# Five blocks of on-chip buffers change places: the same tiles at other byte offsets

## The reference

```python
x   = x + 0.5 * m_x[2] * swiglu(modulate(rmsnorm(x, norm_g[0]), m_x[0], m_x[1]), ffn1_w1, ffn1_w2)
ctx = ctx + 0.5 * m_c[2] * swiglu(modulate(rmsnorm(ctx, norm_g[0]), m_c[0], m_c[1]), ffn1_w1, ffn1_w2)
px = modulate(rmsnorm(x, norm_g[1]), m_x[3], m_x[4]) @ w_in      # q, k, v, gate, u, vg
pc = modulate(rmsnorm(ctx, norm_g[1]), m_c[3], m_c[4]) @ w_in    # only k, v are used
ret = retention_readout(bidir_retention(rope(q), rope(k), v, states from ctx), gate)
gm  = gelu(u) * (W_s @ layernorm(gelu(vg)) + b_s)                # per chunk of 128 tokens
x = x + m_x[5] * (concat([ret, gm]) @ w_out)
x = x + 0.5 * m_x[8] * swiglu(modulate(rmsnorm(x, norm_g[2]), m_x[6], m_x[7]), ffn2_w1, ffn2_w2)
out = rmsnorm(x, final_g)
```

## Time and profile before

| | us |
|---|---|
| median of three runs | 2045.24 |
| profiled execution, its own time | 2042.7 |
| its span, first to last instruction | 2040.9 |
| TensorE busy in the span | 1998.3 (98%) |
| VectorE busy | 1268.1 (62%) |
| ScalarE busy | 758.4 (37%) |
| GpSimd busy | 497.5 (24%) |
| mean granted TensorE clock | 0.992 of full |

### The profile page before, as it was taken

One profiled execution on the slowest core, in us unless ns is written; L12 is line 12 of the kernel. 1 busy time (PEld: TensorE's weight loads), 2 busy tenths in 40 slices (PEclk: granted clock), 3 DMA queues, 4 the chain that ended last, 5 costly groups with the idle time before them and its releaser, 6 DMA issues.

```text
span 2040.9 us, 26021 instructions
## 1 busy us (share of the span) xinstructions
PE 1998.3 (98%) x10112; PEld 1691.4 (83%) x10112; DVE 1268.1 (62%) x1887; ACT 758.4 (37%) x1098; POOL 497.5 (24%) x311
## 2 busy tenths in 40 slices
PE   8999999999999998999999999999999999999997
PEld 5999988888888887888989898877788888888886
DVE  5987766556788678676454324468556555555555
ACT  4333533333333344445121221445333333334342
POOL 1000033333212204014223232555333421220001
PEclk9999999999999999999999999999999999999998
DMA  8874426666555786833101011121666644466664
GB/s 330 343 267 147 155 78 230 203 194 234 201 189 213 262 297 193 268 113 117 42 21 42 31 42 62 62 83 57 201 196 222 212 155 160 160 216 192 192 194 155
DMA packets 108762, 343.52 MB, mean 168 GB/s; under 512 B 11488, under 2 KB 20960, under 8 KB 90464
## 3 DMA queue, kind: packets, MB, share of 16 engines
q1 hardware_dynamic: 108640, 341.85, 49.1%
HBM read 267.36 MB, written 74.45 MB: 167 GB/s over the span
## 4 chain that ended last, share of the span: by engine, by line
PE 85%; issue 5%; DVE 5%; ACT 2%; DMA 1%; POOL 1%; SPq 0%; DVEq 0%; POOLq 0%; ACTq 0%
PE PS L2146 12%; PE PS L2147 12%; PE PS L2148 12%; PE PS L1988 8%; PE PS L1989 8%; PE PS L1990 8%; PE PS L2188 5%; PE PS L2189 5%; PE PS L2190 5%; PE PS L2104 4%; DVE WVL L1579 1%; PE PS L2364 1%; PE PS L2045 1%; DMA WR<-w_units 1%; DVE DG L1328 1%
## 5 line engine op out<-in xcount | busy, mean ns | idle before, releaser
L2146 PE MATMUL PS<-HH,WVH 128*128 128x512 f32 x672 | 262.5, 391 | 0.0
L2148 PE MATMUL PS<-HH,WVL 128*128 128x512 f32 x672 | 261.6, 389 | 0.0
L2147 PE MATMUL PS<-HL,WVH 128*128 128x512 f32 x672 | 261.5, 389 | 0.0
L1988 PE MATMUL PS<-HH,WH 128*128 128x512 f32 x416 | 164.9, 396 | 2.7 <-DVE WL L1770 2.7
L1990 PE MATMUL PS<-HH,WL 128*128 128x512 f32 x416 | 162.0, 389 | 0.0
L1989 PE MATMUL PS<-HL,WH 128*128 128x512 f32 x416 | 161.9, 389 | 0.0
L1579 DVE TENSOR_TENSOR WVL<-WR,WVH 128x512 fp32r<-128x512 f32 x160 | 115.5, 722 | 69.3 <-ACT WVH L1006 67.8
L2148 PEld LDWEIGHTS PS<-HH,WVL 128*128 128x128 f32 x672 | 126.1, 188 | 26.5
L2146 PEld LDWEIGHTS PS<-HH,WVH 128*128 128x128 f32 x672 | 126.2, 188 | 26.3 <-ACT U L1038 0.4
L2147 PEld LDWEIGHTS PS<-HL,WVH 128*128 128x128 f32 x672 | 126.2, 188 | 25.9
L1625 DVE TENSOR_TENSOR HL<-HLF,HH 128x1024 fp32r<-128x1024 f32 x76 | 106.0, 1404 | 60.0 <-ACT HH L1054 59.4
(11 more groups left out here) (282 smaller groups left out, 4933.6 us busy)
## 6 DMA issues: line engine op xcount, KB each, us to landing
WR<-w_units SPq DMA_DIRECT2D x89, 1024.0 KB, 5.7
gated<-HB SPq DMA_DIRECT2D x44, 512.0 KB, 6.6
down_weight_sums<-WB SPq DMA_DIRECT2D x22, 1024.0 KB, 3.8
gated_sums<-TBF SPq DMA_DIRECT2D x22, 768.0 KB, 4.2
AW<-ada_units SPq DMA_DIRECT2D x12, 1024.0 KB, 13.3
HLF<-down_weight_sums SPq DMA_DIRECT2D x46, 256.0 KB, 3.3
W2RB<-w_units SPq DMA_DIRECT2D x22, 512.0 KB, 3.6
WB<-w_units SPq DMA_DIRECT2D x22, 512.0 KB, 3.6
```

Of the source, the lines that this page charges most:

```text
L1988: pe.matmul(dst, wh, xh, start=first, stop=False)
L2146: pe.matmul(bank[:, :], wh, xh, start=first, stop=False, skip_group_check=True)
L2147: pe.matmul(bank[:, :], wh, xl, start=False, stop=False, skip_group_check=True)
L2148: ins = pe.matmul(bank[:, :], wl, xh, start=False, stop=k == 3, skip_group_check=True)
```

## The change

The five blocks are placed in another order. Nothing else differs: no instruction, no wait, no transfer, no size. The whole diff:

```diff
@@ -158,8 +158,7 @@
         def at(name, shape, dt, offset):
             return nc.alloc_sbuf_tensor_at(name, shape, dt, offset=offset)
 
-        R = 192
-        top = [R + 77824]
+        top = [192]
 
         def keep(name, shape, dt):
             n = 4 * int(np.prod(shape[1:]))
@@ -167,10 +166,7 @@
             top[0] += n
             return at(name, shape, dt, top[0] - n)
 
-        HIGHS = top[0]
-        HH = keep("HH", [P, KT, SEQ], F32R)
-        LOWS = top[0]
-        HL = keep("HL", [P, KT, SEQ], F32R)
+        X = keep("X", [P, KT, SEQ], F32)
         W = top[0]
         WR = keep("WR", [P, 2, KT, UC], F32)
         WH = keep("WH", [P, 2, KT, UC], F32R)
@@ -191,7 +187,12 @@
         LG = keep("LG", [P, 8], F32)
         IDX = keep("IDX", [P, Z_END], F32)
         Z = keep("Z", [P, 8, Z_END], F32)
-        X = keep("X", [P, KT, SEQ], F32)
+        R = top[0]
+        top[0] += 77824
+        LOWS = top[0]
+        HL = keep("HL", [P, KT, SEQ], F32R)
+        HIGHS = top[0]
+        HH = keep("HH", [P, KT, SEQ], F32R)
```

## The result

The changed kernel takes 2046.61 us (median of 20 runs, 2043.59 to 2048.88); the kernel before, run beside it, takes 2043.13 us (20 runs, 2040.36 to 2046.26). The ratio is 1.0014 with an interval of 1.0008 to 1.0020: slower by 2.9 us of 2043 (1.6 to 4.1). The forecast was no change. The profiled execution took 2048.38 us with a span of 2046.6 us, 5.7 us longer than the span of the earlier trace rows. An execution that fell to a far lower granted clock (one of `b64ctx` at 2229.66 us, one of the kernel before beside it at 2501.26 us) is in no ratio.

What follows compares the result with a forecast made beforehand. TensorE was taken as the bound, busy for 1998.3 of 2040.9 us. TensorE's pace, other engines and transfers summed as 0 + 0 + 0 on the median, giving 2045.2 us, range 2041.0 to 2049.5 us.

Steps and rivals of the forecast that it cites:

- the first term of the sum: TensorE's pace in ring and mixer: same step at all homes, taken as 0, at most 3.0 us either way.
- Three ways only, and TensorE's pace is one of them: Time can change only by TensorE's pace, other engines' instructions on the chain (143 us), or transfers there (some 20 us).
- Another step, by even 1 ns, breaks the first term and is worth 10 us: Check on ring and mixer: matmul starts must stay 226.7 to 226.9 ns apart.
- The other engines, 0: ScalarE's splits (1060 ns) and VectorE's low parts (1225 ns) keep their lengths; 0, at most 1.4 us either way.
- The transfers, 0: Loads on the chain land as before, WR in 5.6 to 5.8 us; 0, near bound 0.5 us, far 7.2 us.
- The pair of `gated` loads: Check on transfers: the 256 KB loads into the 76 KB block and HL land within 0.2 us of each other.
- The wait of the block period: TensorE's wait for `U<-U,PS`, 5 times and 4.0 us before; expected between 3 and 8 times.
- the two rivals that live there: Block period: slower, more waits, 2050.4 to 2054.8 us, chance 0.06; faster, waits go, 2041.2 us, chance 0.04.
- the transfers' one: Rival: all loads on the chain take 42% longer, 7.2 us, 2052.4 us; chance 0.03.
- The end of SBUF: Rival: HH reaches into space set aside for DMA descriptors, slowing its accesses; 3.0 us, 2048.2 us; chance 0.01.
- The clock: One half-speed stretch of 6.8 us more or less costs 3.4 us, about the three runs' spread of 3.3 us.

Runs made afterwards that it cites:

- b64ctx: Kernel before with the W block and the context's tiles in R each 64 bytes higher; 2048.64 us against 2044.25, ratio 1.0018.
- a64: Changed kernel with R, HL and HH 64 bytes further, so they differ from W by 0 modulo 256; ratio 1.0000 to the kernel before.
- atail: Changed kernel with the 3,520 bytes of small tables moved to the very end, behind HH; ratio 1.0002 to the kernel before.
- r64: Kernel before with 64 bytes left free between R and everything else; 2051.42 us against 2043.30, ratio 1.0042.
- m1_steps: Micro kernel without the layer: 48 fp32r matmuls at each of 21 weight offsets, 512 and 256 columns; 226.7 to 234.4 and 113.3 to 120.0 ns a step.

## Why the prediction was wrong

**The step that failed is the first term of the sum**: "Three pairings of homes at distances from zero to over 100,000 bytes have one pace ... I take 0: the nearest rows are equal." The rows were right and the conclusion wasn't. In all three pairings of the earlier trace rows the blocks' bases were 192 modulo 4096 and the operands inside them begin at multiples of 512 bytes: the distances varied by tens of thousands of bytes, but only in multiples of 512. The rows could not say anything on low address bits, and the change moved just these for one block. The table of offsets ahead of the prediction holds the hint: 32,960 minus 85,632 is no multiple of 256, while every difference of the bases `R`, `HIGHS`, `LOWS` and `W` before is. The size of the term was then capped by the reading error of the stretches, 0.3 ns a step; it was 6.4 ns on 1,248 matmuls, and -2.7 and -2.1 ns on 2,016 others.

Point by point:
- *Three ways only, and TensorE's pace is one of them*: right. Within the interval the steps account for the whole loss (3.1 us of 2.9, 1.6 to 4.1).
- *"Another step, by even 1 ns, breaks the first term and is worth 10 us"*: the test was the right one and found the cause at once, but the price assumed all 10,112 matmuls. Two classes of 256 columns went the other way and gave 4.9 of 8.0 us back.
- *The other engines, 0*: right; the splits have 1060 and 1059 ns, the low parts 1225 ns.
- *The transfers, 0*: right; `WR` lands in 5.8 us (5.7). The pair of `gated` loads is 0.3 us apart, where 0.2 was set as the bound, because `DRAW` became faster, not `HLF` slower.
- *The wait of the block period*: 5 times, 4.1 us, as before. Neither of the two rivals that live there happened, nor did the transfers' one.
- *The end of SBUF*: refuted by `a64` and `atail`.
- *The clock*: it set the scatter as described, and put 2.6 us on the 3.1 us of the layout between the two profiled executions. A forecast of "within 0.2%" would have stood on the size, 1.0014; what moved is that 20 runs of each resolve 0.06%, finer than the 0.2% that I had taken as the limit. The kernel is slower beyond its interval, and the reason is one that I had put at nothing.

The missing rival was one mechanism: *the blocks' distance changes in its low bits, and the two operand streams of a matmul meet differently*. It could not be priced from the rows before, because none had unequal low bits in a long run; the honest bound on that term was open, not 3.0 us.

## What to carry to other kernels

When buffers move, compare the addresses of each matmul's two operands modulo 256 bytes, not their distance: for fp32r matmuls with 512 moving columns keep them equal (226.7 against 233.3 ns a step), and with 256 columns try an unequal pair such as 64 bytes (117.8 against 120.0), measured in the kernel itself. Short blocks with unequal addresses also slow their equal neighbours (`r64`: 230.8 ns over blocks of 12), so price the neighbours too. An alignment pad ahead of each large block makes a reorder free, as `a64` shows with 64 bytes. A row is evidence only for what varies in it: before "all pairings have one pace" is used, write the pairings' addresses down and look at which bits differ.

## What the runs showed of the hardware

- The step of fp32r matmuls depends on the low eight bits of the distance between TensorE's two SBUF operands, with nothing else running: `m1_steps`, 226.7 ns at multiples of 256 bytes and 233.4 at 64 more. The Trainium skill (SBUF — State Buffer, section "Who interferes with whom") states that "PE and ACT never wait on anyone". No run here speaks against that as far as other engines go; what they show is that its own operand streams are not independent of each other.
- Even at equal addresses an fp32r matmul of 512 columns takes 226.7 ns, 13.3 ns more than 512 columns at one per cycle of 2.4 GHz, 213.3 ns. The Trainium skill (TensorE: Matmul & The Clock Gate, section "Wait — 56ns, not 53.3ns?") gives 2.5 ns on top, 215.7 ns. The trace has that figure for another form: the plain float32 products `PR,W2RB` of 256 columns step by a median of 216 ns. For fp32r it does not hold in any of these runs.
- What ran before counts. At 256 columns one address pattern settled at 117.8 ns in one run and 113.3 ns in another, and the better one of a micro kernel need not come in the kernel. Equal addresses at 512 columns behind unequal ones take up to ten steps to come back to 226.7 ns: `r64`, `m1_steps`.
